# Decode tokens that follow the prompt through out-projection and MLP of a hybrid decoder step

## The chip, the cores and the metric

The kernel runs on one core of one Trainium2 chip. The metric is the device time of one execution in microseconds (us), the median of several runs. It is an inference step of a two-layer decoder for a prompt of 512 tokens and 8 decode tokens at once, with the same weights.

## The reference, cut to what matters

Both groups of tokens pass the same layers. The change lies in layer 0: the mixers' output is multiplied by `w_out`, added to the residual behind a norm, and followed by an MLP with a squared ReLU.

```python
def even_mixer(h, w_in, ..., w_out, lam_init, gla_s0, attend):
    ...
    a_out = rmsnorm(attend(da_q, da_k, da_v), g_da) * (1.0 - lam_init)
    ...
    o = rmsnorm(o.astype(h.dtype), g_gla) * jax.nn.silu(g_og).reshape(B, T, GLA_HEADS, GLA_DV)
    mix = jnp.concatenate([a_out.reshape(B, T, DA_V), o.reshape(B, T, GLA_V)], axis=-1)
    return (mix @ w_out).astype(h.dtype), da_k, da_v, s_new.astype(h.dtype)
...
def sq_relu_mlp(h, w_up, w_down):
    return jnp.square(jax.nn.relu(h @ w_up)) @ w_down
...
        yp = yp + rmsnorm(mp, g[1])
        ys = ys + rmsnorm(ms, g[1])
        yp = yp + rmsnorm(sq_relu_mlp(rmsnorm(yp, g[2]), w_up[layer], w_down[layer]), g[3])
        ys = ys + rmsnorm(sq_relu_mlp(rmsnorm(ys, g[2]), w_up[layer], w_down[layer]), g[3])
```

`attend` of a decode token reads a paged cache of 4096 past keys and values (`diff_attn_sample`), 128 MB over the 8 tokens: 64 chunks of 1 MB of keys and 64 of values. D_MODEL is 1024, the MLP's inner width 4096, all of it fp32.

## The kernel before, in words

Activations lie with the features on the 128 partitions (8 tiles of features, `KT`) and the tokens in columns: T = 520, the prompt's 512 and behind them the 8 decode tokens. A large product runs in chunks of weights of 1 MB (1024 x 256), each with two tiles of 128 output features. A weight is split in two parts that the fast fp32r matmul takes, `W_hi` (ACT, `split_hi`, L810) and `W_lo` (DVE, `split_lo`, L1285), the activations likewise into `H_hi` and `H_lo` (in the MLP's second product `U_hi` and `U_lo`), and a tile adds W_hi·hi, W_hi·lo and W_lo·hi for 8 k tiles. As a PSUM bank holds 512 columns, each of these is two matmuls of 260 columns in two banks: 48 matmuls in a tile (`step`, L1876 to 1883):

```python
for n, (w, x) in enumerate(((W_hi, hi), (W_hi, lo), (W_lo, hi))):
    for j, half in enumerate(halves):
        t = MM_(PS[:, 2 * bank + j, 0:HALF], w[:, ch.slot, k, cols], x[:, k, half],
                start=k == 0 and n == 0, stop=k == KT - 1 and n == 2)
```

The chunks follow each other: 13 of the input projection, C_OUT0 with 4 of the out-projection (8 tiles), C_MLP0 with 32 of the first MLP (64 tiles, in four groups of four up and four down chunks), C_IN1 with 8, C_OUT1 with 4 and C_MLP1 with 32 of layer 1. They come by SP's queue (`RAW`). In front of the MLP stands an opening, in which tiles already run in quarters while the norm of the residual is made.

The program is written engine by engine, with semaphores between them, and each engine's order is the order of the code. Work is laid in between by numbered slots (`slot`): the prompt's attention is 16 units, GLA 8 units, and the page cache is worked on in between. `load_order` makes one list of 128 loads of it, k chunks and v chunks: `UNIT_STEPS` says how many k chunks an attention unit takes (with two v chunks), `GLA_STEPS` the same for a GLA unit (three v chunks each). POOL issues these loads as indirect DMAs (L747) into a ring of six 1 MB buffers `KV` once the chunk that lay there is used. A k chunk costs DVE three passes (a product, L1364, and two sums, L1352 and L1366) and POOL a product (L680); a v chunk is four fp32 matmuls of 32 x 512 on four column groups of PE (`v_chunks`, L2074), with weights `PM` that POOL copies (L693) from the softmax scores; its use increments `v_used`. POOL further makes the powers of the norms (`power`, L704 and L708) and zeroes `ACC`. SP brings back the residual X (2 MB, put aside while two of the six buffers lie in its place) once `v_used` is at 62, ahead of a load of the out-projection's weights.

After the GLA units the tail follows: the last v chunks, the decode tokens' softmax sums (`smz_done`), Exp on ACT, the past output (`past_output`), squares, their sum (`new_sq`), the root (`new_root`) and the split of the decode tokens' columns into H_hi and H_lo. PE waits for it (`new_ready`) in front of the out-projection.

## Time and profile before

| | us |
|---|---|
| median of 3 runs | 1544.59 |
| lowest and highest run | 1537.25, 1545.81 |
| profiled execution, span from first to last instruction | 1541.8 |
| PE busy (matmuls) in it | 1406.3 |
| DVE, ACT, POOL busy | 882.3, 516.7, 328.7 |

No separate time is given for the profiled execution: its span stands for it, and lies 2.8 us under the median. A busy PE is an engine that has a matmul in it, not one at its peak. The two stretches of the change are the units of attention and GLA (190 to 515 us), and out-projection with MLP (540 to 971 us).

### The profile page before, as it was taken

To read this page: it belongs to the slowest core of one execution; us is meant where nothing else is said; L and a number is where in the kernel's file an instruction comes from. 1 tells how busy PE (TensorE), PEld (TensorE's weight loads), DVE (VectorE), ACT (ScalarE), POOL (GpSimd) and SP (SyncE) were. 2 spreads that over 40 slices of the span, in tenths; PEclk is the share of its full clock that TensorE was granted. 3 is DMA by queue.
4 is the path that set the end of the run, shared out by engine and by line. 5 is a ranking of instruction groups with operands and counts; after the bars stand their busy time and mean duration, and the time that the engine had idled before them with its cause. 6 is when DMAs were issued, how large, how long until landed. Compare 5 with 4: busy or idle time off the path is not lost.

```text
span 1541.8 us, 26106 instructions
## 1 busy us (share of the span) xinstructions
PE 1406.3 (91%) x11324; PEld 1266.3 (82%) x11324; DVE 882.3 (57%) x1156; ACT 516.7 (34%) x839; POOL 328.7 (21%) x264
## 2 busy tenths in 40 slices
PE   4999957788778698999999999899989999999997
PEld 3999933345334398999999999899989999999997
DVE  3398978766988526624435343689556344353443
ACT  3323254433423424312212122469443122131233
POOL 1085768865777100000000000000000000000000
PEclk8999979877676799999999999999999999999999
DMA  9477699988989831232322322222212323223211
GB/s 320 137 264 232 236 327 382 369 324 326 346 322 346 300 109 55 86 106 83 97 97 82 99 94 83 83 83 83 85 55 88 105 83 101 92 83 103 90 55 56
DMA packets 126856, 249.32 MB, mean 162 GB/s; under 512 B 5251, under 2 KB 107415, under 8 KB 110096
## 3 DMA queue, kind: packets, MB, share of 16 engines
q0 software_dynamic: 18432, 134.23, 22.9%
q1 hardware_dynamic: 103616, 107.13, 21.5%
q10 hardware_dynamic: 4696, 6.32, 1.3%
q8 instruction: 89, 1.46, 0.4%
q14 instruction: 23, 0.19, 0.0%
HBM read 239.99 MB, written 7.73 MB: 161 GB/s over the span
## 4 chain that ended last, share of the span: by engine, by line
PE 58%; issue 25%; DVE 7%; POOL 4%; DMA 3%; ACT 3%; ACTq 0%; POOLq 0%; DVEq 0%
PE PS L1881 46%; PE PS L2074 2%; POOL PROD L680 2%; DMA KV<-in_cache_v,CIDX 2%; DVE SC L1352 1%; PE PS L2216 1%; POOL KV L747 1%; DVE ST L1584 1%; PE PS L2061 1%; PE PS L2158 1%; DMA XSIN<-in_x_sample 1%; PE PS L1865 1%; PE PS L2179 1%; PE PS L2116 1%; PE PS L1975 1%
## 5 line engine op out<-in xcount | busy, mean ns | idle before, releaser
L1881 PE MATMUL PS<-H_hi,W_hi 128*128 128x260 f32 x1936 | 397.7, 287 | 16.7 <-DVE H_lo L1327 9.7
L1881 PE MATMUL PS<-H_hi,W_lo 128*128 128x260 f32 x1936 | 393.4, 285 | 0.0
L1881 PE MATMUL PS<-H_lo,W_hi 128*128 128x260 f32 x1936 | 393.0, 285 | 0.0
L1881 PEld LDWEIGHTS PS<-H_hi,W_hi 128*128 128x128 f32 x1936 | 303.2, 191 | 22.3 <-issue 17.7
L1881 PEld LDWEIGHTS PS<-H_hi,W_lo 128*128 128x128 f32 x1936 | 301.9, 191 | 0.0
L1881 PEld LDWEIGHTS PS<-H_lo,W_hi 128*128 128x128 f32 x1936 | 301.7, 191 | 0.0
L1285 DVE TENSOR_TENSOR W_lo<-RAW,W_hi 128x2048 fp32r<-128x2048 f32 x90 | 208.2, 2313 | 125.9 <-ACT W_hi L810 125.8
L810 ACT ACTIVATE W_hi<-RAW 128x2048 fp32r<-128x2048 f32 x90 | 171.8, 1909 | 266.1 <-PE PS L1881 265.5
L1881 PE MATMUL PS<-U_hi,W_lo 128*128 128x260 f32 x1024 | 206.4, 283 | 0.0
L1881 PE MATMUL PS<-U_lo,W_hi 128*128 128x260 f32 x1024 | 206.0, 283 | 0.0
L1881 PE MATMUL PS<-U_hi,W_hi 128*128 128x260 f32 x1024 | 206.0, 282 | 0.0
L680 POOL TENSOR_TENSOR PROD<-KV,QB 128x1024 f32<-128x1024 f32 x64 | 152.0, 2375 | 120.4 <-DVE SC L1352 91.5
L1717 DVE TENSOR_TENSOR ACC<-ACC,PS 128x520 f32<-128x520 f32 x64 | 44.6, 697 | 201.4 <-PE PS L1881 201.4
L1881 PEld LDWEIGHTS PS<-U_hi,W_hi 128*128 128x128 f32 x1024 | 157.9, 189 | 0.0
L1881 PEld LDWEIGHTS PS<-U_hi,W_lo 128*128 128x128 f32 x1024 | 157.9, 188 | 0.0
L1881 PEld LDWEIGHTS PS<-U_lo,W_hi 128*128 128x128 f32 x1024 | 157.4, 188 | 0.0
L753 POOL MEMSET ACC<- 128x4160 f32 x2 | 7.1, 3572 | 637.3 <-DVE TMP L1310 637.3
L1124 ACT ACTIVATE UF<-SQ 128x520 f32<-128x520 f32 x64 | 40.8, 639 | 253.2 <-DVE SQ L1683 253.2
L2074 PE MATMUL PS<-KV,PM 128*32 128x512 f32 x512 | 88.2, 777 | 23.4 <-DMA KV<-in_cache_v,CIDX 13.6
L1683 DVE SCALAR_TENSOR_TENSOR SQ<-PS,RS 128x520 f32<-128x520 f32 x64 | 44.6, 700 | 109.2 <-PE PS L1881 109.2
L1364 DVE TENSOR_TENSOR PROD<-KV,PS 128x1024 f32<-128x1024 f32 x64 | 77.5, 1210 | 9.0 <-ACT QB L866 8.9
L747 POOL DMA_INDIRECT KV<-in_cache_k,CIDX x64 | 70.4, 1100 | 53.8 <-DVE TMP L1310 23.1
(304 smaller groups left out, 1433.8 us busy)
## 6 DMA issues: line engine op xcount, KB each, us to landing
RAW<-in_w_up SPq DMA_DIRECT2D x32, 1024.0 KB
RAW<-in_w_down SPq DMA_DIRECT2D x32, 1024.0 KB
...
```

Of the source, the lines that this page charges most:

```text
L680: nc.gpsimd.tensor_tensor(PROD[:, 1], KV[i % RING][:, 2:4, :], QB[:, None, b % 2, :].to_broadcast([P, 2, 512]), ALU.mult).then_inc(prod1_r ...
L747: po.indirect_dma_start(KV[i % RING].rearrange("p n f -> p (n f)"), None, cache[kind], bass.IndirectOffsetOnAxis(ap=CIDX[:, n:n + 1], axis ...
L810: A(W_hi[:, ch.slot], RAW[:, ch.slot], ACT.Copy).then_inc(w_hi_ready, 1)
L1124: A(UF[:, i], RL[:, i], ACT.Square).then_inc(uf_ready, 1)
L1285: V.tensor_tensor(W_lo[:, ch.slot], RAW[:, ch.slot], W_hi[:, ch.slot].bitcast(F32), ALU.subtract).then_inc(w_lo_ready, 1)
L1352: V.tensor_reduce(k_scores(n, 1), PROD[:, 1].rearrange("p n (j d) -> p n j d", d=DH), AX.X, ALU.add).then_inc(prod1_used, 1)
L1364: V.tensor_tensor(PROD[:, 0], KV[i % RING][:, 0:2, :], PS[:, None, 6 + b % 2, :].to_broadcast([P, 2, 512]), ALU.mult).then_inc(k_used, 1)
L1584: V.scalar_tensor_tensor(ST[:, hp, state(tb, n + 1)], ST[:, hp, state(tb, n)], DECC[:, hp, 8 * tb + n:8 * tb + n + 1], update(n, slice(0, ...
L1683: V.scalar_tensor_tensor(pair(RL[:, i]), tile_banks(ch, i), 0.0, pair(RS[:, 1]), ALU.max, ALU.mult).then_inc(banks_free[ch.par[i]], 1)
L1717: V.tensor_tensor(pair(ACC[:, m]), pair(ACC[:, m]), banks(ch.par[i]), ALU.add).then_inc(banks_free[ch.par[i]], 1)
L1881: t = MM_(PS[:, 2 * bank + j, 0:HALF], w[:, ch.slot, k, cols], x[:, k, half], start=k == 0 and n == 0, stop=k == KT - 1 and n == 2)
L2074: t = MM_(PS[32 * pos:32 * pos + 32, 4, :], PM[:, part % 2, at:at + 32], KV[i % RING][:, pos, :], start=n % 32 == 0, stop=n % 32 == 31)
```

## The change

The prompt passes the out-projection and the first MLP alone. A tile of the chunks from C_OUT0 up to C_IN1 (`prompt_only`, 72 tiles) has 24 matmuls of 512 columns into one bank; splits and evictions of these chunks leave the decode tokens' columns out. The decode tokens follow behind the tiles of the MLP (`sample(t)`, with t the tile, on PE, ACT and DVE): t=4 softmax sums and past output, 5 attention, 7 and 8 norm, 10 and 11 four chunks of `w_out`, 13 fold, 15 to 19 norms, and from t=21, with a period of 8, per group four up chunks (behind two tiles), a fold, and four down chunks, at the end a fold and the residual (behind tiles 53 to 56). A chunk is 8 fp32 matmuls with the tokens' values as weights of 32 columns (8 tokens, four times) and 256 columns of the model's weights (`sample_products`, L2169), on four column groups of PE; `folds` adds up the four and turns them back to features on partitions (8 matmuls of 128 x 128 by 8 columns). POOL loads these weights again, 36 chunks of 1 MB in rows of 1 KB by `dma_start` (L814), into a ring of three buffers; a load waits until the chunk before in its buffer is used (`w_used`). SP restores X once the last cache chunks that lie in its place (v 48 and 49) are used.

The cache's chunks are spread anew: in the attention units by turns 1 and 2 k chunks (8 more), in the GLA units by turns 2 and 1 (12 in place of 20) with two v chunks each (16 in place of 24), then v chunks 48 to 51, and 52 to 63 in pairs behind the first six tiles of the out-projection (`values_behind`). The weights `PM` have a second buffer. POOL zeroes ACC ahead of the fourth weight load.

PE's order in front of the out-projection. Before: the last two v chunks, the past output's sums (L2082), the norm's sum (L2197) and the first tile, which waits for `new_ready`.

```order
L2074 MATMUL PS<-KV_69,PM 32x512 [waits pm_ready,kv_loaded0]
L2074 MATMUL PS<-KV_69,PM 32x512 x3
L2074 MATMUL PS<-KV_69,PM 32x512 [waits pm_ready,kv_loaded1]
L2074 MATMUL PS<-KV_69,PM 32x512 x3
L2082 MATMUL PS<-CONST,OG_111 128x32 [waits og_copied]
L2082 MATMUL PS<-CONST,OG_111 128x32 x3
L2197 MATMUL PS<-MM,ONES 128x64 [waits new_sq,hf_ready,gs_v_used]
L1881 MATMUL PS<-H_hi,W_hi 128x260 [waits banks_free1,h_ready,w_lo_ready,new_ready]
L1881 MATMUL PS<-H_hi,W_hi 128x260
L1881 MATMUL PS<-H_lo,W_hi 128x260 x2
L1881 MATMUL PS<-H_hi,W_lo 128x260 x2
```
In the change PE has v chunks 50 and 51 there, the last norm of GLA (L2359), and then the tile, without that wait and 512 columns wide.

```order
L2344 MATMUL PS<-KV_69,PM_99 32x512 [waits pm_ready,kv_loaded0]
L2344 MATMUL PS<-KV_69,PM_99 32x512 x3
L2344 MATMUL PS<-KV_69,PM_99 32x512 [waits pm_ready,kv_loaded1]
L2344 MATMUL PS<-KV_69,PM_99 32x512 x3
L2359 MATMUL PS<-NDG,OT 128x128 [waits nd_ready,gs_v_used,st_ready]
L2359 MATMUL PS<-NDG,OT 128x128 [waits nd_ready]
L2086 MATMUL PS<-H_hi,W_hi 128x512 [waits h_ready,banks_free1,w_lo_ready]
L2086 MATMUL PS<-H_lo,W_hi 128x512
L2086 MATMUL PS<-H_hi,W_lo 128x512
```
The past output and the norm's sum stand behind tiles of the MLP now. In the out-projection two v chunks lie between two tiles:

```order
L2086 MATMUL PS<-H_hi,W_hi 128x512 [waits h_ready]
L2086 MATMUL PS<-H_lo,W_hi 128x512
L2086 MATMUL PS<-H_hi,W_lo 128x512
L2344 MATMUL PS<-KV_69,PM_99 32x512 [waits pm_ready,kv_loaded2]
L2344 MATMUL PS<-KV_69,PM_99 32x512 x3
L2344 MATMUL PS<-KV_69,PM_99 32x512 [waits pm_ready,kv_loaded3]
L2344 MATMUL PS<-KV_69,PM_99 32x512 x3
L2086 MATMUL PS<-H_hi,W_hi 128x512 [waits banks_free0]
L2086 MATMUL PS<-H_lo,W_hi 128x512
```
And in the MLP two chunks of `w_up` between two tiles, L2169, with XH as the tokens' values:

```order
L2086 MATMUL PS<-H_hi,W_lo 128x512
L2086 MATMUL PS<-H_hi,W_hi 128x512
L2086 MATMUL PS<-H_lo,W_hi 128x512
L2086 MATMUL PS<-H_hi,W_lo 128x512
L2169 MATMUL PS<-KV_69,XH 32x256 [waits kv_loaded0,operand_ready]
L2169 MATMUL PS<-KV_69,XH 32x256 x7
L2169 MATMUL PS<-KV_69,XH 32x256 [waits kv_loaded1]
L2169 MATMUL PS<-KV_69,XH 32x256 x7
L2086 MATMUL PS<-H_hi,W_hi 128x512 [waits banks_free0]
L2086 MATMUL PS<-H_lo,W_hi 128x512
```
These are each behind a wait on the load, and the first also on the tokens' values (`operand_ready`).

DVE's order in the attention units, before (a k chunk is L1352, L1364, L1366):

```order
L1546 RECIPROCAL RR<-SM 128x2 [waits ex_done]
L1520 TENSOR_TENSOR PR<-PS,BIAS 128x1024 [waits at_done,sc_done]
L1523 TENSOR_REDUCE MX<-PR 128x2 [waits sc_used]
L1529 TENSOR_SCALAR OTC<-PS 128x128 [waits o_copied]
L1538 SCALAR_TENSOR_TENSOR NRS<-NSQ,NRS 128x1 [waits root_done]
L1352 TENSOR_REDUCE SC_78<-PROD 128x2x8 [waits prod1_ready]
L1364 TENSOR_TENSOR PROD<-KV_70,PS 128x1024 [waits kv_loaded5]
L1366 TENSOR_REDUCE SC_78<-PROD 128x2x8 [waits k_used]
L1404 TENSOR_REDUCE ROWSUM<-SC_77 128x8 [waits soft_done,dve_step]
L1546 RECIPROCAL RR<-SM 128x2 [waits ex_done]
```
and in the change, in a unit that takes two (the lines are L1472, L1484 and L1486):

```order
L1666 RECIPROCAL RR<-SM 128x2 [waits ex_done,dve_step]
L1640 TENSOR_TENSOR PR<-PS,BIAS 128x2x128 [waits at_done,sc_done]
L1643 TENSOR_REDUCE MX<-PR 128x2 [waits sc_used]
L1649 TENSOR_SCALAR OTC<-PS 128x128 [waits o_copied]
L1658 SCALAR_TENSOR_TENSOR NRS<-NSQ,NRS 128x1 [waits root_done]
L1472 TENSOR_REDUCE SC_78<-PROD 128x2x8 [waits prod1_ready]
L1484 TENSOR_TENSOR PROD<-KV_70,PS 128x1024 [waits kv_loaded5]
L1486 TENSOR_REDUCE SC_78<-PROD 128x2x8 [waits k_used]
L1472 TENSOR_REDUCE SC_78<-PROD 128x2x8 [waits prod1_ready,dve_step]
L1484 TENSOR_TENSOR PROD<-KV_69,PS 128x1024 [waits kv_loaded0]
L1486 TENSOR_REDUCE SC_78<-PROD 128x2x8 [waits k_used]
L1472 TENSOR_REDUCE SC_78<-PROD 128x2x8 [waits prod1_ready,dve_step]
```
DVE's third pass of one k chunk is followed by the three of the next, ahead of the unit's next step.

The diff, cut:

```diff
     IN_STEPS, PRE_STEPS = 2, (3, 3)
-    UNIT_STEPS = [1] * 16
-    GLA_STEPS = [3, 3, 3, 3, 3, 3, 2, 0]
+    UNIT_STEPS = [1, 2] * 8
+    GLA_STEPS = [2, 1] * 4
     GLA_SLOT = len(UNIT_STEPS) + 13
+    OUT_SLOT = GLA_SLOT + 17
...
-            take("kvkvkv" if n == 3 else "kvkvv" if n == 2 else "vvv")
+            take("kvkv" if n == 2 else "kvv")
...
-        return order
+        return order + [("w", n) for n in range(36)]
...
+    ALL_SIX, SAMPLE_RING = 114, 3
+
+    def buffer(i):
+
+        return i % RING if i < ALL_SIX else (i - ALL_SIX) % 4 if i < LOADS else (i - LOADS) % SAMPLE_RING
...
+    def prompt_only(ch):
+
+        return C_OUT0 <= ch.static < C_IN1
...
-                sp.wait_ge(v_used, 62)
+                for i in range(ALL_SIX - RING, ALL_SIX):
+                    if BUFFER[i] >= 4:
+                        freed(sp, i)
                 sp.dma_start(X[:].rearrange("p k t -> p (k t)"), xsave).then_inc(x_saved, 16)
...
+        def sample_weights(n):
+
+            if n < 4:
+                return stage_dram(a["w_out_even"][0], 0, slice(256 * n, 256 * n + 256))
+            c, j = SAMPLE_CHUNKS[n - 4]
+            if c[0] == "up":
+                return stage_dram(a["w_up"][0], 0, slice(1024 * c[1] + 256 * j, 1024 * c[1] + 256 * j + 256))
+            return a["w_down"][0].rearrange("(q r p) n -> p q r n", p=P, r=KT)[:, c[1], :, 256 * j:256 * j + 256]
+
+        used = 0
+        for i, (kind, n) in enumerate(ORDER):
+            if (kind, n) == ("w", SAMPLE_RING):
+                zero_acc(0)
+            if BEFORE[i] is not None:
+                while used <= BEFORE[i]:
+                    use(used)
+                    used += 1
...
+            if kind == "w":
+                po.dma_start(weights_of(n), sample_weights(n)).then_inc(kv_loaded[BUFFER[i]], 16)
+            else:
+                po.indirect_dma_start(KV[BUFFER[i]].rearrange("p n f -> p (n f)"), None, cache[kind],
+                                      bass.IndirectOffsetOnAxis(ap=CIDX[:, n:n + 1], axis=0)).then_inc(kv_loaded[BUFFER[i]], 16)
...
             for n, (w, x) in enumerate(((W_hi, hi), (W_hi, lo), (W_lo, hi))):
+                if prompt_only(ch):
+                    t = MM_(PS[:, bank, :], w[:, ch.slot, k, cols], x[:, k, 0:SEQ], start=k == 0 and n == 0, stop=k == KT - 1 and n == 2)
+                    continue
                 for j, half in enumerate(halves):
...
+        def sample_products(n, op, bank, fresh):
+
+            i = place("w", n)
+            pe.wait_ge(kv_loaded[BUFFER[i]], LANDED[i])
+            for r in range(2):
+                for c in range(4):
+                    k = 4 * r + c
+                    t = MM_(PS[32 * c:32 * c + 32, bank, 256 * (n % 2):256 * (n % 2) + 256], op[:, k], weights_of(n)[:, k],
+                            start=fresh and r == 0, stop=r == 1, skip_group_check=True)
+            t.then_inc(w_used, 1)
+
+        def folds(n):
+
+            pe.wait_ge(part_copied, min(2 * n + 1, 10))
+            for k in range(KT):
+                t = MM_(PS[:, 6, 64 + 8 * k:72 + 8 * k], SE[:, P * k:P * k + P], FOLD[:, 0:8], start=True, stop=True)
+            t.then_inc(fold_done, 1)
...
+            if t in (10, 11):
+                pe.wait_ge(operand_ready, 1)
+                for n in range(2):
+                    sample_products(2 * (t - 10) + n, XM, 3 if t == 10 else 5, True)
...
+            g, at = group_step(t)
+            if at in (0, 1):
+                pe.wait_ge(operand_ready, 2)
+                for n in range(2):
+                    sample_products(4 + 8 * g + 2 * at + n, XH, 2 + 2 * at, True)
+            if at == 3:
+                folds(g + 1)
+            if at in (5, 6):
+                pe.wait_ge(operand_ready, g + 3)
+                for n in range(2):
+                    sample_products(4 + 8 * g + 4 + 2 * (at - 5) + n, XU[:, g % 2], 3 if at == 5 else 5, g == 0 and n == 0)
...
+        v_chunks(48, 4)
         pe.wait_ge(st_ready, 64)
-        pe.wait_ge(k_used, 64)
-        v_chunks(56, 2)
-        normalise(23)
-        pe.wait_ge(ssum_ready, 8)
...
-        v_chunks(58, 6)
-        past_output(1)
-
-        pe.wait_ge(gs_v_used, N_SAMPLE)
...
-        pe.wait_ge(new_ready, 1)
-        stage(C_OUT0, 4, 1)
+        pe.wait_ge(gs_v_used, N_SAMPLE)
+        normalise(23)
+
+        def values_behind(t):
+
+            slot(OUT_SLOT + t)
+            if t < 6:
+                v_chunks(52 + 2 * t, 2)
+
+        stage(C_OUT0, 4, 1, values_behind)
```

## Rows read from the trace of the kernel before

**Rows 1.** Busy time by stretch (us, x instructions), PE clock, DMA share, GB/s.
```profile
core 0: us, PE busy (x) PEld busy (x) DVE busy (x) ACT busy (x) POOL busy (x), PEclk, DMA share, GB/s
190.00:366.00 176.00, 133.16 (x754) 72.14 (x754) 130.72 (x188) 76.86 (x223) 127.68 (x114) 0.81 0.91 347
366.00:515.00 149.00, 114.93 (x851) 60.08 (x854) 120.09 (x216) 51.26 (x174) 102.06 (x91) 0.69 0.91 342
515.00:540.20 25.20, 13.73 (x82) 5.53 (x74) 16.11 (x44) 11.47 (x25) 3.89 (x6) 0.72 0.71 247
540.20:618.90 78.70, 73.68 (x672) 72.57 (x673) 33.99 (x39) 27.69 (x40) 3.57 (x1) 0.94 0.25 78
618.90:970.90 352.00, 351.99 (x2932) 351.86 (x2936) 151.12 (x160) 86.69 (x77) 0.00 (x0) 1.00 0.28 91
```

**Rows 2.** The chain of waits from the out-projection on: start us, us, what.
```profile
540.22 47.72 PE PS L1881 x384
...
618.91 351.99 PE PS L1881 x2928
```

**Rows 3.** Costliest groups of DVE, 190 to 366 us, shapes apart.
```profile
L1366 DVE TENSOR_REDUCE SC<-PROD 128x16 f32<-128x1024 f32 x23 | 28.1, 1221 | 0.8
L1364 DVE TENSOR_TENSOR PROD<-KV,PS 128x1024 f32<-128x1024 f32 x23 | 27.8, 1210 | 0.0
L1352 DVE TENSOR_REDUCE SC<-PROD 128x16 f32<-128x1024 f32 x22 | 26.7, 1214 | 1.4 <-POOL PROD L680 1.4
```

**Rows 4.** Waits of DVE, 190 to 366 us: total us, times, longest.
```profile
DVE PR L1520 <- PE PS L2061: 23.8, 10, 5.1
```

**Rows 5.** Busy time by stretch, the stretch in which the DMA is fullest.
```profile
224.00:296.00 72.00, 53.56 (x325) 25.44 (x323) 58.36 (x85) 34.47 (x115) 56.84 (x55) 0.89 0.97 378
```

**Rows 6.** The chain of waits, GLA units: start us, us, what.
```profile
374.35 3.71 PE PS L2158 x32
...
393.46 7.75 DMA KV<-in_cache_v,CIDX
...
468.47 1.93 PE PS L2158 x16
...
483.14 8.06 DMA KV<-in_cache_v,CIDX
...
503.67 1.93 PE PS L2158 x16
```

**Rows 7.** Timeline of the tail, 528 to 540.5 us: start us, us, engine, line.
```profile
528.03 0.69 DVE L1609 TENSOR_TENSOR H_lo<-HTMP,H_hi 128x512 fp32r<-128x512 f32 x1
...
529.99 1.89 ACT L810 ACTIVATE W_hi<-RAW 128x2048 fp32r<-128x2048 f32 x1
...
535.68 2.28 DVE L1285 TENSOR_TENSOR W_lo<-RAW,W_hi 128x2048 fp32r<-128x2048 f32 x1
```

**Rows 8.** The chain of waits, a gate product of layer 1.
```profile
1007.54 1.75 PE PS L2216 x8
```

**Rows 9.** The chain of waits, a v chunk and a small product.
```profile
342.08 0.99 PE PS L2074 x8
343.08 1.87 PE PS L2044 x16
```

**Rows 10.** The view of DMA issues: median us from issue to landing.
```profile
KV<-in_cache_v,CIDX POOLq DMA_INDIRECT x64, 8.0
```

**Rows 11.** Groups from 366 to 515 us: POOL's issue of a cache load.
```profile
L747 POOL DMA_INDIRECT KV<-in_cache_v,CIDX x28 | 27.8, 994 | 8.0 <-POOL PROD L680 3.5 <-PE PS L2074 2.1 <-issue 1.7
```

**Rows 12.** DMA queues of the page: packets, MB, share of 16 engines.
```profile
q0 software_dynamic: 18432, 134.23, 22.9%
q1 hardware_dynamic: 103616, 107.13, 21.5%
```

**Rows 13.** Groups of DVE from 618.9 to 970.9 us.
```profile
L1688 DVE CAST U_hi<-UF 128x520 fp32r<-128x520 f32 x32 | 13.8, 431 | 20.5 <-ACT UF L1124 20.4
```

More of the change, by code:

```diff
@@ L523, in trunk, with weights_of, group_step @@
     LOADS = 128
+    ALL_SIX, SAMPLE_RING = 114, 3
+    def buffer(i):
+        return i % RING if i < ALL_SIX else (i - ALL_SIX) % 4 if i < LOADS else (i - LOADS) % SAMPLE_RING
+    BUFFER = [buffer(i) for i in range(len(ORDER))]
+    BEFORE = [max([j for j in range(i) if BUFFER[j] == BUFFER[i]], default=None) for i in range(len(ORDER))]
+    LANDED = [16 * BUFFER[:i + 1].count(BUFFER[i]) for i in range(len(ORDER))]
+    def weights_of(n):
+        return KV[BUFFER[place("w", n)]].rearrange("p n f -> p (n f)").rearrange("p (k n) -> p k n", k=KT)
+    SAMPLE_CHUNKS = [((what, g), j) for g in range(4) for what in ("up", "down") for j in range(4)]
+    SAMPLE_MLP, SAMPLE_PERIOD = 21, 8
+    SAMPLE_END = SAMPLE_MLP + 3 * SAMPLE_PERIOD + 6
+    def group_step(t):
+        g, at = divmod(t - SAMPLE_MLP, SAMPLE_PERIOD)
+        return (g, at) if 0 <= g < 4 and t >= SAMPLE_MLP else (None, None)
     UNITS = [(h, qb) for h in range(HEADS) for qb in range(4)]
@@ L685, in weights @@
             b, half = divmod(part, 2)
+            PM = PM_AT[part // 8]
             if part == 0:
@@ new lines, in part, with fold_square @@
+        def part(n, banks_):
+            act.wait_ge(w_used, 4 if n == 0 else 36 if n == 9 else 8 * ((n - 1) // 2) + 6 + 2 * ((n - 1) % 2))
+            if n >= 1:
+                act.wait_ge(fold_done, (n + 1) // 2)
+            for i, bank in banks_:
+                t = A(SE[:, 512 * i:512 * i + 512], PS[:, bank, :], ACT.Copy)
+            t.then_inc(part_copied, 1)
+        def fold_square(n, src):
+            if n >= 1:
+                act.wait_ge(new_summed, n + 1)
+            A(by_tile(E1), src, ACT.Square).then_inc(new_sq, 1)
@@ L2202, in _ @@
         mlp(0, C_MLP0, 2)
+        pe.wait_ge(sample_moved, 4)
         sum_squares(3)
```

416 lines of the change are left out of this document (271 added, 145 removed).

## The prediction

> **What bounds the kernel now.** I read the busy time by stretch first, then the chain of waits, then the groups. Over the two stretches in which the change makes PE's tiles narrower PE never rests: 73.7 of 78.7 us and 351.99 of 352.0 us, with DVE at 151 of 352 and DMA at 0.28 [rows 1]. The chain says the same: 47.72 us for the 384 matmuls of the out-projection's 8 tiles, then 351.99 us in one piece for 2928 matmuls, 61 tiles [rows 2]. So a microsecond of PE work added or removed there is a microsecond of the kernel, and all other engines have room. From 190 to 515 us it is otherwise: PE is busy 133 of 176 and 115 of 149 us, DVE 131 and 120, POOL 128 and 102, DMA 0.91 of its time, in both [rows 1]. No engine is full; the units of attention and GLA are chains through PE, ACT and DVE, and the page cache's chunks (one k chunk costs three DVE passes and one POOL product) are laid in between. From 515 to 540.2 us there is the tail, where PE waits for the decode tokens' softmax, norm and split.
>
> **The change, part by part.**
>
> *Attention units, +16.* Eight units take one k chunk more. A chunk costs DVE 1.22 + 1.21 + 1.21 = 3.64 us [rows 3], eight of them 29. DVE waits there 23.8 us in 10 waits for scores of PE [rows 4], half of which or a little more the new work can fill: +14 by DVE, +29 if nothing is absorbed. By DMA: 8.4 MB more, at the 378 GB/s of the fullest stretch [rows 5] 22 us, less what the share still leaves (0.91 against 0.97 of 176 us, 11 us): +11. With some friction between the two I take **+16**, bounds +11 and +29.
>
> *GLA units, −31.* The first stretch of state products starts at 374.35, that of the sixth unit at 468.47, that of the eighth at 503.67 [rows 6]: 18.8 us for a unit with 3 k and 3 v chunks, and 35.2 for one such and the one with 2 and 2 (16.4 for the latter; by one chunk's DVE time less, 18.8 − 3.64, it would be 15.2, and I take 15). The last, with none, needs 515 − 503.67 = 11.3. A unit with one k chunk is put at 12.5, between 11.3 and 15. Before: 515 − 366 = 149, of which 8.4 lie ahead of 374.35. Now 8.4 + 4 × 15 + 4 × 12.5 = 118: **−31**. The chain has waits on a v chunk's DMA of 7.75 and 8.06 us there [rows 6], which fall due to fewer chunks in the queue; that speaks for more (−38), a unit that can't get under 14 for less (−20).
>
> *Tail, −8.* PE started the out-projection at 540.22 [rows 2]. The prompt's last H_lo is done at 528.72; then ACT began W_hi late (529.99 for 1.89) and DVE W_lo at 535.68 for 2.28, behind the decode tokens' chain [rows 7]. Now the wait on that chain is gone from PE's first row of the out-projection. 528.7 − 0.7 (ACT is free when DVE does the last H_lo) + 1.9 + 2.3 = 532.2: **−8**, bounds −6 and −11 (the last norm's square roots come earlier on ACT, but four v chunks stand on PE before them).
>
> *Tiles 24 × 512, −41.* A matmul of 260 columns takes 351.99/2928 = 0.1202 us, so a pair 0.2404. What does one of 512 columns take? The nearest row is the fp32 gate product of layer 1: 8 records in 1.75 us, 0.219 each [rows 8], and such a record streams its 260 columns twice, 520. Per column that is 0.421 ns, so 512 take 0.2155. The other bound is that the 260s pay per column (0.1202/260 × 512 = 0.2367). I take 0.2155, since the row with as many columns gives it. 72 tiles × 24 × (0.2404 − 0.2155) = 43; two of the three opening tiles wait anyway, **−41**. Bounds −6 and −43. The Trainium skill, "TensorE: Matmul & The Clock Gate", section "Wait — 56ns, not 53.3ns?", says a matmul costs N/2.4 GHz and some 2.5 ns more. The row of the 260s disagrees, 120.2 against 110.8 ns. By the rule a tile would now take 24 × 215.8 = 5.18 us, as I have it, but before 48 × 110.8 = 5.32, and the saving would be 10 us, not 41.
>
> *48 chunks between tiles, +48.* Twelve v chunks move from ahead of the out-projection to behind its tiles, and 36 chunks of re-read weights (4 out-projection, 16 up, 16 down) are new, each with 8 fp32 matmuls of 32 × 256 on four column groups at once. PE's order shows both kinds between tiles, each behind a wait on its load. A v chunk standing alone takes 0.99 us at full clock [rows 9]; a weight chunk has 16 records, four side by side, so four rounds of 512 streamed columns at 0.2155: 0.86, and its end drains like the other's. 48 × 0.99 = **+48**; 48 × 0.86 = 41 is the lower bound.
>
> *Folds and small sums, +14.* A fold is 8 fp32 matmuls, 16 records, with a full weight load and 8 columns. 16 records of that sort (64 × 128 weights, one column) took 1.87 us [rows 9]; six folds +11, and the softmax sums, the past output's sums and the four norm sums **+3**.
>
> *Loads of the re-read weights, +3.* The ring has three buffers, a four of chunks is used by two tiles in a row. The fourth chunk takes the buffer of the first, which comes free behind tile t and is wanted behind tile t+1 and the third chunk: 1.0 + 5.2 + 1.0 = 7.2 us later. A v chunk lands 8.0 us after its issue (median) [rows 10], POOL's issue costs 1.0 [rows 11]; by that each of nine fours would be 1.8 us late, +16. But those loads shared the DMA at 0.91, while here it stands at 0.28; alone, the weight queue needs 21.5% × 1541.8/107.13 = 3.1 us of all engines for one MB [rows 12], which leaves 4 us for issue and what lies around the transfer; so I take most of them in time: **+3**, bounds 0 and +16. POOL has nothing else to do there; the zeroing of ACC is put ahead of the fourth load, long before its use. SP's restore of X waited for v chunk 62 and now for v 48 and 49; it stands ahead of w_out loads in SP's queue and comes earlier. Edits at nothing: DVE's and ACT's decode work between tiles (small operations, 64 columns wide), under PE with DVE idle 200 of 352 us; if a tile's eviction came behind such a step by more than a tile's time (5.2 us) it would cost. The Trainium skill, "SBUF — State Buffer", section "SBUF: two separate sides", warns that a load issued from GpSimd stands still while DVE runs an fp32 SBUF-to-SBUF copy. Such copies run in the MLP, 32 of U_hi at 0.43 us [rows 13]; no row shows whether they hold a load up. By the page each four could be late by one of them, 9 × 0.43 = 4 us more than my sum, and it adds to B's chance.
>
> **Sum.** Front +16 − 31 − 8 = −23. PE stretch −41 + 48 + 14 + 3 = +24. Together +1; against the traced execution 1541.8 + 1 = 1543. That span lies 2.8 under the median of the runs, 1544.59; I forecast **1544**, for the median.
>
> **Rivals.**
> *A, the front gives more* (1529). The attention units take their chunks for +11, GLA falls by 38, the tail by 11: −38, with +24 behind it −14. For it: two DMA waits of 8 us each in the GLA chain, with fewer chunks to fetch. Against: of DVE's 120 us of work in GLA 20 × 3.64 = 73 are chunks, and not all of that is on the chain.
> *B, loads late* (slower, 1557 to 1596). POOL's issue costs 1.0 us for a cache chunk whose packets are 134.23 MB/18432 = 7.3 KB; the weight queue's are 107.13 MB/103616 = 1.0 KB [rows 12], so a chunk of weights has seven to eight times as many. If POOL pays by the piece, 7.8 us an issue, a group's eight chunks need 63 us of POOL, while its 8 tiles and 8 chunks take PE 50: +13 for each of four groups, +52 (1596). If only landing is as the cache's, +16, so +13 against my sum (1557). It decides from issue and landing over 7.2 us. For it: nothing in the trace has POOL issuing small rows. Against: slack elsewhere in the ring.
> *C, attention pays in full* (1557): DVE's 29 us land in the chain since the waits it could fill are at the wrong units: +13.
> *D, columns alone set PE's price* (1579): a tile saves 0.09 us, not 0.58.
> *E, nothing of it bites* (1544): gains and costs go unseen, the opening of the MLP or another wait swallowing both.
>
> **How the numbers follow.** Half a per cent, 7.7 us, is about what a measurement tells from no change. The forecast's case has 0.42: its terms wander by some 9 us around +0, so 0.15 faster, 0.22 same, 0.05 slower. A 0.24, all faster. B 0.14 and D 0.05, slower. C 0.09, of which 0.03 same. E 0.06, same. Faster 0.39, same 0.31, slower 0.30. The rule on the clock's page, by which the tiles save 10 and not 41, would give 1575; I give it 0.01 of D's 0.05, since the row of the 260s says otherwise. The range holds the forecast's own (1530 to 1557), A's with its bounds and B's and C's lower parts: 1521 to 1568.
>
> **What would show it.** Tiles of 24 matmuls at 5.17 us, 0.2155 a piece, under MLP 0; at 0.2367 a piece D is right. PE between two tiles at 0.9 to 1.0 us per chunk, with no wait on KV of the weights; B would show as waits of PE on the DMA of w_up or w_down, or as POOL busy for microseconds at each issue. The stretch of attention units 158 us long with DVE at nine tenths; GLA's starts of state products 15 and 12.5 us apart in turn; the out-projection starting near 517. The forecast is wrong if MLP 0 with the out-projection is not some 24 us longer, or the front not some 23 us shorter.

## The result and the profile after

The changed kernel takes 1589.49 us (median of 4 runs, 1586.40 to 1592.71) against 1542.71 us for the kernel before: the ratio is 1.0305, 95% interval 1.0279 to 1.0331. It is 47 us slower than before and 45 us over the forecast of 1544, whose range went up to 1568. The profiled execution has a span of 1586.1 us, so 44.3 us more than that of before.

The chain of waits of the changed kernel shows where PE's time goes now (start us, us, what; L2086 is the tile's matmuls, L2169 a chunk of re-read weights, L2177 a fold):

```profile
531.51 8.52 PE PS L2086 x24
634.25 16.83 PE PS L2086 x72
668.06 1.86 PE PS L2169 x32
669.93 5.79 PE PS L2086 x24
688.95 1.68 PE PS L2177 x16
771.02 7.37 DMA KV<-in_w_down
826.05 8.21 DMA KV<-in_w_down
936.63 8.03 DMA KV<-in_w_down
970.25 44.71 PE PS L2086 x192
1014.96 1.95 PE PS L2070 x64
```

The out-projection starts at 531.51, not at 540.22, and the MLP's end (the norm's first sum, L2070) comes at 1014.96, not 970.90 [rows 2]. So in these two profiles the front (all that stands ahead of the out-projection) gave 8.7 us, and out-projection and MLP took 483.5 us in place of 430.7, 52.8 more, where 24 were forecast; the rest of the program is as long as it was (571.1 and 570.9 us). Three tiles in a row take 16.83 us, eight take 44.71: 5.6 us each, 0.233 us a matmul of 512 columns. That is the row to keep in mind: the sum had 0.2155.

Busy time by stretch, with the columns of [rows 1]:

```profile
190.00:366.00 176.00, 124.49 (x639) 65.04 (x637) 143.29 (x194) 71.73 (x204) 133.88 (x116) 0.76 0.93 348
531.50:1015.00 483.50, 476.34 (x2664) 362.69 (x2668) 195.05 (x253) 126.02 (x141) 48.55 (x47) 0.99 0.53 174
```

PE is busy 476 of 483.5 us: still the bound, as before. DVE from 190 to 366 us rose from 131 to 143 of 176 us, and its waits for scores stayed (from 190 to 390 us, as the attention units end 28 us later):

```profile
DVE PR L1640 <- PE PS L2331: 21.6, 10, 5.4
```

23.8 us before [rows 4], 21.6 now in the longer stretch, 10 waits in both: the added k chunks did not fill them. The loads of the re-read weights, by the page's view of DMA issues (KB each, median us to landing) and POOL's timeline (start us, us):

```profile
KV<-in_w_up POOLq DMA_DIRECT2D x16, 1024.0 KB, 7.7
KV<-in_w_down POOLq DMA_DIRECT2D x16, 1024.0 KB, 8.3
```

```profile
771.02 0.88 POOL L814 DMA_DIRECT2D KV<-in_w_down  x1 [24.31 <-PE PS L2169]
```

POOL's issue of a load in rows of 1 KB costs 0.88 us here and at most 1.00 in any of the 36, no more than one of the cache's [rows 11]. Landing takes 7.7 to 8.3 us (medians of `w_up` and `w_down`) against the 7.2 that the ring leaves, and PE waits for it in three places.

### The profile page after: what moved, and what is told of

Its sections match the earlier page's. It is cut to its first block, busy times and chain, and to the rows that moved or that the text cites. A ratio compares the mean times of both kernels' runs of the same rounds, so it can differ in the third digit from the quotient of the medians.

```text
span 1586.1 us, 24121 instructions
## 1 busy us (share of the span) xinstructions
PE 1446.0 (91%) x10274; PEld 1201.7 (76%) x10274; DVE 886.8 (56%) x1184; ACT 527.3 (33%) x858; POOL 363.1 (23%) x301
## 4 chain that ended last, share of the span: by engine, by line
PE 56%; issue 25%; DVE 9%; POOL 4%; ACT 3%; DMA 3%; POOLq 0%; ACTq 0%; DVEq 0%
PE PS L2086 24%; PE PS L2089 18%; PE PS L2344 3%; POOL PROD L724 3%; PE PS L2169 2%; DVE SC L1472 2%; DMA KV<-in_w_down 1%; DVE ST L1704 1%; PE PS L2428 1%; PE PS L2483 1%; PE PS L2177 1%; PE PS L2245 1%; POOL KV L816 1%; DVE SC L1486 1%; PE PS L2070 1%
## 5 line engine op out<-in xcount | busy, mean ns | idle before, releaser
L2089 PE MATMUL PS<-H_hi,W_hi 128*128 128x260 f32 x1296 | 267.0, 288 | 10.0 <-DVE H_lo L1447 6.5
L2089 PE MATMUL PS<-H_hi,W_lo 128*128 128x260 f32 x1296 | 263.4, 285 | 0.0
L2089 PE MATMUL PS<-H_lo,W_hi 128*128 128x260 f32 x1296 | 263.3, 285 | 0.0
L1919 DVE TENSOR_TENSOR ACC<-ACC,PS 128x512 f32<-128x512 f32 (+1 forms) x64 | 44.3, 692 | 202.5 <-PE PS L2089 103.3
L2086 PE MATMUL PS<-H_hi,W_hi 128*128 128x512 f32 x320 | 130.6, 408 | 15.5 <-DVE W_lo L1405 12.1
L2086 PE MATMUL PS<-H_hi,W_lo 128*128 128x512 f32 x320 | 128.0, 400 | 0.0
L2086 PE MATMUL PS<-H_lo,W_hi 128*128 128x512 f32 x320 | 127.5, 398 | 0.0
L1884 DVE SCALAR_TENSOR_TENSOR SQ<-PS,RS 128x512 f32<-128x512 f32 (+1 forms) x64 | 44.3, 695 | 116.1 <-PE PS L2086 61.3
L2089 PE MATMUL PS<-U_hi,W_lo 128*128 128x260 f32 x512 | 103.2, 283 | 0.0
L2089 PE MATMUL PS<-U_lo,W_hi 128*128 128x260 f32 x512 | 103.0, 283 | 0.0
L2089 PE MATMUL PS<-U_hi,W_hi 128*128 128x260 f32 x512 | 103.0, 282 | 0.0
L2086 PE MATMUL PS<-U_hi,W_hi 128*128 128x512 f32 x256 | 102.6, 401 | 0.0
L2086 PE MATMUL PS<-U_hi,W_lo 128*128 128x512 f32 x256 | 101.3, 396 | 0.0
L2086 PE MATMUL PS<-U_lo,W_hi 128*128 128x512 f32 x256 | 100.8, 394 | 0.0
```

What stands on the lines that cost most here:

```text
L1884: V.scalar_tensor_tensor(tile_cols(ch, RL[:, i]), tile_banks(ch, i), 0.0, tile_cols(ch, RS[:, 1]), ALU.max, ALU.mult).then_inc(banks_free[ ...
L1919: V.tensor_tensor(tile_cols(ch, ACC[:, m]), tile_cols(ch, ACC[:, m]), tile_banks(ch, i), ALU.add).then_inc(banks_free[ch.par[i]], 1)
L2086: t = MM_(PS[:, bank, :], w[:, ch.slot, k, cols], x[:, k, 0:SEQ], start=k == 0 and n == 0, stop=k == KT - 1 and n == 2)
```

## The experiments

Twelve kernels ran. The theory after the result (P): an fp32r matmul of 512 columns costs 233 ns, not 215.5, and this alone is 72 x 24 x 17.5 ns = 30 us, about all of what the stretch took beyond its forecast (52.8 against 24). The rivals: late loads (B, as in the prediction), and the added traffic slowing PE's matmuls (called C in this section; it is not the prediction's C, attention in full).

**What a matmul costs, alone.** `e1_widths_alone` puts sections of 96 matmuls behind PE's last work in the kernel before:

```diff
+        def w_of(i):
+            return WT[:, P * (i % 16):P * (i % 16) + P]
+
+        def x_of(i, n):
+            return XT[:, 512 * (i % 7):512 * (i % 7) + n]
...
+        for i in range(96):
+            MM_(PS[:, bank(i), :], w_of(i), x_of(i, 512), start=first(i), stop=last(i))
...
```

`WT` and `XT` are `W_hi` and `W_lo` flattened; `bank(i)` changes every 24 matmuls.

> The kernel before, with eleven sections of 96 matmuls each behind PE's last work, all other engines idle. A new 128x128 weight load stands before each. Theory P (an fp32r matmul pays 0.449 ns a column and 3.4 ns more, from 120.0 ns at 260 and 233 ns at 512 in the traces): 512 columns 233 ns in all fp32r sections of that width, whichever bank they write, 384 columns 176, 260 columns 120, 256 columns 118, 128 columns 61. Rival Q (the 512s are slow since one bank takes matmul upon matmul): 233 with one bank for 24 in a row, 216 with banks by turns. Rival C (the other engines or the DMA slow PE's reads or writes): 216 in all sections of 512 here, since all else is idle. The fp32 section (256 columns, two passes) at 108 a record and the bf16 section at 216 would say that it is the fp32r form that costs, 233 in bf16 that it is the width. The time of the whole is before's plus some 200 us and says nothing.

The timeline of PE (start us, us from the first start to the last end, form, count); a section's starts lie 96 apart from the next one's:

```profile
1571.05 21.92 PE L2280 MATMUL PS<-W_lo,W_hi 128*128 128x512 f32 x96
1592.81 21.92 PE L2282 MATMUL PS<-W_lo,W_hi 128*128 128x512 f32 x96
1614.57 16.83 PE L2284 MATMUL PS<-W_lo,W_hi 128*128 128x384 f32 x96
1631.24 11.67 PE L2286 MATMUL PS<-W_lo,W_hi 128*128 128x256 f32 x96
1642.74 11.56 PE L2288 MATMUL PS<-W_lo,W_hi 128*128 128x260 f32 x96
1654.14 10.83 PE L2290 MATMUL PS<-W_lo,W_hi 128*128 128x128 f32 x96
...
1686.67 41.60 PE L2294 MATMUL PS<-W_lo,W_hi 128*128 128x256 f32 x192
1728.33 20.67 PE L2296 MATMUL PS<-XBF,WBF 128*128 128x512 bf16 x94
1748.64 22.12 PE L2298 MATMUL PS<-W_lo,W_hi 128*128 128x512 f32 x96
```

(1592.81 − 1571.05)/96 = 0.2267 us at 512 columns, in one bank as with banks by turns (L2282): rival Q falls. 384 columns cost (1631.24 − 1614.57)/96 = 0.1736, 256 cost 0.1199, 260 cost 0.1187, 128 cost 0.111, where theory P had 0.061 for the last. From 256 to 512 that is 0.417 ns a column, full speed, and 13.4 ns on top of N/2.4: on these rows theory P's form (nearly all by the column) falls. But 13.4 ns isn't a constant of every width: at 260 columns only 10.4 ns lie on top, at 128 it is 58. Nor is it there at the lower clock: the starts of the first section (L2278) lie 427 ns apart while its granted clock is 0.50 (1.2 GHz), which is 512/1.2.

The fp32 product has two records a matmul, 192 in all, and they start 0.216 us apart (median), twice the 108 that I expected; 256 columns in a record of fp32 so take the time of 512 in a bf16 matmul, also 0.216. So at 512 streamed columns it is the fp32r form that pays; my row for the price, an fp32 product [rows 8], was of a kind that doesn't. 0.2267 is still not 0.233: 6 ns were open.

**The rest of it: where the moving rows start.** `e8_operands_alone` takes the tile's operands apart:

```diff
+            MM_(PS[:, bank(i), :], w_of(i), XT[:, 520 * (i % 6):520 * (i % 6) + 512], start=first(i), stop=last(i))
...
+            MM_(PS[:, bank(i), :], (W_hi, W_hi, W_lo)[i % 3][:, 1, (i // 3) % KT, P:2 * P], (U_hi, U_lo, U_hi)[i % 3][:, (i // 3) % KT, 0:512], start=first(i), stop=last(i))
```

> The kernel before with seven sections of 96 fp32r matmuls of 512 columns behind PE's last work, all else idle: which part of the operands takes them from 226.7 ns (first run) to the 233 of the tiles. In order: as in the first run (226.7); the moving rows 2080 bytes apart, not 2048; weights taken in rows of 1024 bytes out of W_hi; the tile's own order of weights (W_hi twice, then W_lo) with moving rows from W_hi; that order with the tile's own moving tiles (U_hi, U_lo, U_hi); plain weights with U_hi's rows; the same tile in rows 2048 bytes apart. Theory A (addresses of the moving rows): 233 in the second, fifth and sixth, 227 in the last. Theory W (the weights' order or layout): 233 in the third, fourth and fifth. Theory N (what else runs on the chip): 227 everywhere.

```profile
1550.74 24.55 PE L2280 MATMUL PS<-W_lo,W_hi 128*128 128x512 f32 x96 [13.56 <-ACT WBF L1250]
1575.12 22.46 PE L2282 MATMUL PS<-W_lo,W_hi 128*128 128x512 f32 x96
1597.42 21.94 PE L2284 MATMUL PS<-W_lo,W_hi 128*128 128x512 f32 x96
```

Rows 2080 bytes apart: (1597.42 − 1575.12)/96 = 0.2323. The mean spacing of the seven sections, from the trace: 227 (the median; this section begins at the lower clock), 232.2, 226.9, 232.2, 232.5, 234.1, 226.9 ns. Theory A holds: the second, the fifth and the sixth are slow, the last (the same U_hi, rows of 2048 bytes) is not. The fourth is slow too, but its moving rows also lay 2080 bytes apart, so it says of the weights' order only that it adds nothing to the second. Weights' layout and order do nothing that shows, and all this with everything else idle, so nothing is left for other engines.

`e9_addresses_alone` moves the start of rows 2048 bytes apart, by s = 4, 8, 16, 32, 64, 128 and 256 columns of 4 bytes:

```diff
+            MM_(PS[:, bank(i), :], w_of(i), XT[:, 512 * (i % 6) + 4:512 * (i % 6) + 516], start=first(i), stop=last(i))
...
```

> The kernel before with fourteen sections of 96 fp32r matmuls behind PE's last work, all else idle. First as in the first run (512 columns, moving rows 2048 bytes apart: 226.7 ns). Then the same rows moved by 16, 32, 64, 128, 256, 512 and 1024 bytes. If the price hangs on the start's alignment, the sections up to some power of two stand at 229 to 237 and the rest at 227: at 64 bytes and more if rows of 64 bytes matter, only at 1024 if it is larger blocks. If instead all stand at 227, it is not the start but that starts differ from one matmul to the next (rows 2080 bytes apart) that costs. Then six sections of pairs with the same weights, in two banks: 260 + 260 in rows of 2080 bytes as the kernel before has them (120 expected each, as there), 256 + 256 aligned (119.9 if the fixed part holds), 260 twice from the same aligned start (118.7 as in the first run), 260s at rows of 2112 and starts of 1056 bytes, 260s at rows of 2176 and starts of 1024 bytes, and 264s at 1024 in rows of 2080. Differences over 1 ns in the 260s would be worth 90 x 2 x 48 x 1 ns = 8 us to the kernel before.

```profile
1572.03 22.40 PE L2282 MATMUL PS<-W_lo,W_hi 128*128 128x512 f32 x96
1594.27 22.57 PE L2284 MATMUL PS<-W_lo,W_hi 128*128 128x512 f32 x96
1616.67 22.14 PE L2286 MATMUL PS<-W_lo,W_hi 128*128 128x512 f32 x96
1638.65 22.46 PE L2288 MATMUL PS<-W_lo,W_hi 128*128 128x512 f32 x96
1660.95 21.93 PE L2290 MATMUL PS<-W_lo,W_hi 128*128 128x512 f32 x96
1682.71 21.92 PE L2292 MATMUL PS<-W_lo,W_hi 128*128 128x512 f32 x96
...
1726.23 11.68 PE L2296 MATMUL PS<-W_lo,W_hi 128*128 128x260 f32 x96
1737.75 11.68 PE L2298 MATMUL PS<-W_lo,W_hi 128*128 128x256 f32 x96
1749.27 11.55 PE L2300 MATMUL PS<-W_lo,W_hi 128*128 128x260 f32 x96
1760.66 11.70 PE L2302 MATMUL PS<-W_lo,W_hi 128*128 128x260 f32 x96
1772.20 11.79 PE L2304 MATMUL PS<-W_lo,W_hi 128*128 128x260 f32 x96
1783.83 12.00 PE L2306 MATMUL PS<-W_lo,W_hi 128*128 128x264 f32 x96
```

Shifted by 16, 32, 64 and 128 bytes: 231.6, 233.4, 228.9, 232.3 ns; by 256, 512 and 1024: 226.7. So a start at a multiple of 256 bytes, counted from the beginning of `W_lo`, is free, and each other one that was tried costs 2 to 7 ns. For the 260s of the kernel before it is another story: in rows of 2080 bytes 120.0 ns, both halves from the same aligned start 118.7, and the two layouts meant to be better 120.2 and 121.1. The aligned 256s take 120.0, more than the aligned 260s; why is open. A 260 + 260 in 2080 is within 1.3 ns of the best that was tried.

`e11_before_aligned` asked this of the whole kernel before:

```diff
-                    t = MM_(PS[:, 2 * bank + j, 0:HALF], w[:, ch.slot, k, cols], x[:, k, half],
+                    t = MM_(PS[:, 2 * bank + j, 0:HALF], w[:, ch.slot, k, cols], x[:].rearrange("p k t -> p (k t)")[:, 512 * k + 256 * j:512 * k + 256 * j + HALF],
```

> The kernel before with the moving operand of every tile's matmuls taken from windows of 260 columns that begin 1024 bytes apart (512k and 512k + 256 of the flattened tile, so partly other tokens' and features' numbers), in all chunks. If the 260s pay for their starts as the 512s do (227 against 233), up to 1.3 ns a matmul (118.7 idle and aligned against 120.0 in the tiles): 8640 x 1.3 = 11 us less than before, 1531. If a 260's 120 ns has nothing to do with addresses: no change, 1542.

1558.85 us, ratio 1.0117 (1.0089 to 1.0145): 16 to 18 us slower, a miss of both theories. The chain has the MLP's piece at

```profile
619.50 357.69 PE PS L1881 x2928
```

0.1222 a matmul against 0.1202. What in these windows costs it (they overlap, and each starts 1024 bytes after the last) is open. It does say that where the moving windows lie can cost this kernel 1%.

`e10_rows_2048` lays out the moving tiles of the prompt-only products in rows of 2048 bytes:

```diff
+    HP_hi, HP_lo = (sb(n, [P, KT, SEQ], F32R, at) for n, at in (("HP_hi", r_h), ("HP_lo", r_h + KT * TB)))
+    UP_hi, UP_lo = (sb(n, [P, KT, SEQ], F32R, at) for n, at in (("UP_hi", r_1), ("UP_lo", r_1 + KT * TB)))
```

> The changed kernel with the moving tiles of the prompt-only products (both halves of H and U) laid out in rows of 512 columns, 2048 bytes apart and starting on 256 bytes, not in rows of 520; nothing else differs. If the start addresses cost what the idle sections show (233 against 226.7 ns at 512 columns), a tile falls from 5.60 to 5.44 us and the whole by 72 x 24 x 6.3 ns = 11 us from the changed kernel's 1589.5, to 1579. If what else runs on the chip makes the 6 ns, tiles stay at 5.60 and the time at 1589.

1584.78 us (ratio to before 1.0273, 1.0221 to 1.0326). The chain:

```profile
641.48 16.45 PE PS L2091 x72
...
971.44 43.62 PE PS L2091 x192
```

A tile takes 5.45 to 5.48 us where it took 5.6; the median spacing of its matmuls under MLP 0 is 227 ns, where it was 232. From the out-projection's start to the MLP's end it is 475.4 us against 483.5, 8 us less. The tiles show the effect of the rows; the whole shows 5 of the expected 11, and the rest is within what the front (below) wanders.

**The width alone.** `e2_before_wide` is the kernel before with the wide tiles (and one matmul more in the opening's third tile, for the bank that it would leave empty):

```diff
+                if C_OUT0 <= ch.static < C_IN1:
+                    t = MM_(PS[:, 2 * bank, :], w[:, ch.slot, k, cols], x[:, k, 0:SEQ], start=k == 0 and n == 0, stop=k == KT - 1 and n == 2)
+                    if bank == THIRD and k == 0 and n == 0:
+                        MM_(PS[:, 2 * bank + 1, 0:HALF], w[:, ch.slot, k, cols], x[:, k, 0:HALF], start=True, stop=True)
+                    continue
```

> The kernel before with the change's wide tiles alone: 24 matmuls of 512 columns in the 72 tiles of out-projection and MLP 0. The decode tokens' columns of these tiles are left out, and nothing is put in their place. Theory P: a tile falls from 5.77 to 5.60 us, 72 x 0.17 = 12 us less than before, about 1530. The prediction's price (0.2155 us a matmul): 5.17 a tile, 41 us less, about 1501.

```profile
543.87 46.66 PE PS L1881 x192
...
620.54 340.64 PE PS L1881 x1464
```

1532.27 us, 0.993 of before (0.990 to 0.996), 10 us less; the MLP's piece fell from 351.99 to 340.64 [rows 2], and from the out-projection's start to the MLP's end it is 417.3 us in place of 430.7. So the price of 0.233 is right for the tile without the change's other parts (340.64/1464), and on rows of 2080 bytes the width gives 10 to 13 us, not 41. Some 6 of them (72 x 24 x 8/2.4 ns, an estimate from full speed by the column) are the eight columns that a pair no longer has. `e7_halves_one_bank` cuts the matmuls in two in the changed kernel:

```diff
+                    for j in range(2):
+                        t = MM_(PS[:, bank, 256 * j:256 * j + 256], w[:, ch.slot, k, cols], x[:, k, 256 * j:256 * j + 256], start=k == 0 and n == 0 and j == 0, stop=k == KT - 1 and n == 2 and j == 1)
```

> The changed kernel with each matmul of 512 columns cut into two of 256, in the same bank. If each fp32r matmul pays a fixed 13.4 ns beside N/2.4 (first run: 226.7 ns at 512, 173.6 at 384, 119.9 at 256, all idle), a tile takes 48 x 0.1199 = 5.76 us or a little more, against 5.60: 72 x 0.16 = 12 us more than the changed kernel, 1601. If the cost goes by the column (theory P of the first run), 48 x 0.1184 = 5.68, 6 us more, 1595. If the 6 ns that the tiles' 512s take beyond the idle 226.7 come from the length of a single matmul, the halves stand at 0.1165 and nothing is lost: 1589.

```profile
639.61 17.05 PE PS L2087 x144
```

1598.48 us, 9 us over the changed kernel; three tiles in 17.05, 5.68 each, 0.1184 a half. That is the tile of the second case, cost by the column, to the last digit, and not the 5.76 of a fixed 13.4 ns. So the numbers of the idle sections on aligned rows don't carry over to these tiles: on rows of 2080 bytes a pair of 256s (236.8) costs only 3.4 ns more than one 512 (233.4), on aligned rows 13 ns more (2 x 119.9 against 226.7). The time, 9 us more, lies between the two cases. Why a 256 isn't slowed by the starts that slow a 512 is open.

**The decode tokens' products and their loads.** `e3_no_weight_loads` and `e4_half_products`:

```diff
-                po.dma_start(weights_of(n), sample_weights(n)).then_inc(kv_loaded[BUFFER[i]], 16)
...
-            pe.wait_ge(kv_loaded[BUFFER[i]], LANDED[i])
```

> The changed kernel without the 36 loads of re-read weights and PE's waits on them; the decode tokens' products run on what lies in the buffers (so their out-projection and MLP of layer 0 are computed from other data). Theory P: tiles stay at 5.60 us, only PE's waits on late loads go, 3 to 4 us: 1586. Rival B (late loads hold the kernel up): 10 us or more less, under 1580. Rival C (the added DMA traffic slows PE's matmuls): tiles near 5.2 us, 30 us less, 1560.

1589.67 us: no gain. From the out-projection's start to the MLP's end it is 480.2 us against 483.5. Of these 3.3 us, 1.4 are the first tile (7.16 against 8.52; its matmuls start 427 ns apart while the granted clock is 0.50, 12 of them in the changed kernel and 5 here, and near 232 ns after). From the MLP's fourth tile on it is 391.3 us against 393.7, so the waits on late loads were worth 2.4 us, near the sum's +3; whatever DVE's copies of U_hi did to these loads is in that. The tiles stayed at 5.6 us with the DMA at 0.30 of its time in place of 0.53:

```profile
540.49 7.16 PE PS L2084 x24
...
540.50:1020.70 480.20, 475.16 (x2664) 362.62 (x2668) 195.00 (x253) 126.03 (x141) 15.93 (x11) 0.99 0.30 97
```

B and C both fall. A gain of 2 us can't be told from nothing in the time: the four runs lie between 1586 and 1594, and in the profiles the front ended at 540.5 here and at 531.5 in the changed kernel.

```diff
-            for r in range(2):
+            for r in range(1, 2):
                 for c in range(4):
...
-                            start=fresh and r == 0, stop=r == 1, skip_group_check=True)
+                            start=fresh, stop=True, skip_group_check=True)
```

> The changed kernel with 4 of the 8 matmuls of each re-read chunk (the other half of the inner dimension is left out of the decode tokens' products). If a chunk costs what its matmuls stream (two rounds of four records at 0.215 us gone of four), 36 x 0.43 = 15.5 us less than the changed kernel, 1574. If a chunk's price is mostly that PE's run of tiles is broken, under 8 us less, over 1581.

```profile
679.16 7.70 DMA KV<-in_w_out_even
...
745.81 1.00 PE PS L2169 x16
746.81 5.79 PE PS L2086 x24
```

1579.41 us, 10 us less, between the two cases. From the out-projection's start to the MLP's end it is 473.1 us, 10.4 less. A pair of chunks fell from 1.86 to 1.00, as priced (18 pairs, 15.5 us), but a third of that came back: PE now waits longer for loads (5.0 us in PE's own waits, against 1.7). With shorter products the ring's buffers are wanted sooner, which would explain it; no run tests that. The 5.79 behind a pair, against 5.6 in a row, is the break: 0.19 us a time.

**The front.** `e5_tables_back` puts eight k chunks back from the attention into the GLA units:

```diff
-    UNIT_STEPS = [1, 2] * 8
-    GLA_STEPS = [2, 1] * 4
+    UNIT_STEPS = [1] * 16
+    GLA_STEPS = [3, 3, 3, 3, 3, 2, 2, 1]
```

> The changed kernel with the k chunks where they were: one in every attention unit, and 3, 3, 3, 3, 3, 2, 2, 1 in the GLA units (20), the v chunks as in the change. If a k chunk costs DVE's 3.64 us on the chain wherever it lies (rival C of the prediction, for both stretches), attention falls by 28 us and GLA rises by 28 to 29: the changed kernel's time within 3 us, 1589. If GLA has more room than attention, its eight chunks cost 15 to 20 us there, and the whole falls to 1577 to 1582. If DVE's waits fill with the chunks in attention only, it rises to 1595 or more.

1581.45 us, 8 us less (ratio to before 1.0261, 1.0222 to 1.0299), as in the second case. In its profile the first mask of GLA is written at 366.9 in place of 401.4 (373.5 in before), and from there to the last unit's it takes 121.9 us in place of 101.8. One profile of each isn't enough here, since the front wanders; more are at hand, as other runs have the same front. Means, in us from the profiles:

| front | profiles | first mask of GLA | from it to the last unit's | from there to the out-projection | out-projection's start |
|---|---|---|---|---|---|
| of before | before, e1, e2, e8, e9 | 372.1 (369.6 to 374.4) | 129.6 (127.5 to 131.6) | 39.1 | 540.8 (537.9 to 543.9) |
| of the change | changed kernel, e3, e4, e7, e10 | 402.3 (401.3 to 403.2) | 105.9 (101.8 to 108.8) | 29.5 | 537.7 (531.5 to 541.7) |
| of e5 | e5, e12 | 370.4 (366.9, 374.0) | 122.0 (121.9, 122.0) | 30.9 | 523.3 (519.7, 526.8) |

So a k chunk cost (402.3 − 370.4)/8 = 4.0 us in attention, all of DVE's 3.64 and more, and (122.0 − 105.9)/8 = 2.0 in GLA. The stretches, the changed kernel's first, then e5's:

```profile
222.00:366.00 144.00, 106.42 (x548) 52.46 (x548) 118.28 (x165) 53.80 (x178) 111.96 (x103) 0.76 0.95 356
401.50:503.00 101.50, 80.50 (x680) 44.88 (x676) 78.64 (x152) 41.84 (x146) 58.24 (x52) 0.75 0.73 272
```

```profile
222.00:366.00 144.00, 115.62 (x688) 60.33 (x688) 110.25 (x172) 64.10 (x214) 110.54 (x109) 0.86 0.96 367
366.90:488.80 121.90, 85.90 (x685) 48.25 (x685) 108.51 (x182) 45.02 (x150) 84.78 (x69) 0.68 0.81 299
```

DVE is busy for 0.77 of the thinned GLA and 0.89 with the chunks back, and for 0.82 of attention with the added chunks and 0.77 without. These shares alone don't tell which stretch has room: 0.77 in both, and a chunk costs twice as much in attention. My reading is that DVE, ACT and PE wait for each other in each attention unit, so that what is laid between delays all of it; no run tests that reading by itself.

`e6_w_hi_early` moves ACT's split in the tail of the kernel before:

```diff
         squares_of(23)
+        split_hi(Chunk(C_OUT0))
         normalise(23)
...
         A(E2[:], E2[:], ACT.Exp).then_inc(mm_exp, 1)
-        split_hi(Chunk(C_OUT0))
```

> The kernel before with one thing moved in its tail: ACT makes W_hi of the out-projection's first chunk behind the squares of the last GLA unit, not between the decode tokens' Exp and the past output's copy. In the chain of before it holds 1.8 us there. Expected 1.8 us less than before, 1540 to 1541, which three rounds will hardly tell from nothing; the trace must show the past output's copy right behind Exp and the out-projection's start 1.8 us sooner after the clamp.

```profile
517.52 1.89 ACT L810 ACTIVATE W_hi<-RAW 128x2048 fp32r<-128x2048 f32 x1
...
531.41 0.24 ACT L1060 ACTIVATE E<-E 128x64 f32<-128x64 f32 x1
...
532.05 0.60 ACT L997 ACTIVATE OG<-PS 128x512 f32<-128x512 f32 x1 [0.40 <-PE PS L2074]
```

1539.34 us, 0.998 of before (0.9958 to 1.0002): the split has left the chain, and from the last GLA unit's mask to the out-projection it is 36.8 us in place of 38.6, the 1.8 expected (38.4 to 40.0 in four more profiles with the front of before). In the time it can't be told from nothing. Of the versions that leave nothing out it is the only one that isn't slower than before; no run found one that is clearly faster.

`e12_rows_and_tables` joins e10 and e5:

```diff
+    HP_hi, HP_lo = ...
-    UNIT_STEPS = [1, 2] * 8
+    UNIT_STEPS = [1] * 16
```

> The two mended together: rows 2048 bytes apart, and the k chunks back in the GLA units as in e5. The savings lie in different stretches and should add: 11 for the rows and 8 for the tables, 1589.5 - 19 = 1570. If the front's saving was chance (e5's front in its profile was 12 us shorter, its median 8), only the rows' part remains, 1579. Both stand clear above the 1542 of the kernel before, because the 36 re-read chunks, the folds and the twelve v chunks stay on PE.

```profile
628.57 16.45 PE PS L2091 x72
```

1575.91 us (1.021 of before, 1.0154 to 1.0266), 13.6 us under the changed kernel: the two add up, 5 and 8 as each alone gave, and so stay 6 short of the 1570 expected, all of it on the side of the rows. It stays 33 us over before.

## Why the prediction was wrong

*Tiles, −41: the step that failed.* The direction was right (one matmul in place of two costs less), the size was off by three to four times. The row that I took by its columns, the gate product, was fp32, and the tiles are fp32r: 512 columns cost 226.7 ns on aligned rows, 233 on rows of 2080 bytes, not 215.5. Measured worth of the width: 10 us in the time of e2, 13 in its stretch. These 29 or so are the larger part of the 45 us by which the time missed. The other bound, 236.7 ns, from the 260s' price by the column, was 3 ns off, and rival D, with 0.05, came closest to what happened. Its price by the column is nearly right for these tiles, as e7 shows, and not in general: on aligned rows a wide matmul saves 13 ns against two of 256, and the addresses of the rows take back half of that. The rule of the Trainium skill, "TensorE: Matmul & The Clock Gate", section "Wait — 56ns, not 53.3ns?", of N/2.4 GHz and 2.5 ns more, agrees with bf16 here (216 ns against 215.8) and with the fp32 records, not with fp32r. By that rule the saving would be 10 us, which hit the measured one, but by luck in part: both of its prices are too low, by 9 ns at 260 columns and 17 at 512. I had weighed the 260s' row against the rule and not asked whether the other row was of the same type.

*48 chunks, +48.* Right: a pair 1.86 and 0.19 for the break, 24 times 2.05 is 49. *Folds and sums, +14*: six folds of 1.68 and some 2 us, about 12. *Loads, +3*: right, 2.4 by e3; POOL's issue (B's 7.8 us) is 0.88.

*Attention, +16: the second step that failed.* It took 28.0 in the profile and 30 on the mean of five, the upper bound: rival C, for which I had 0.09. The chain's rows of waits on scores looked like room and weren't: they stayed at 21.6 us with eight chunks more. Why they stay is argued above, not shown. *GLA, −31, and tail, −8*: −26.4 and −10.2 in the profile, which together is near the −39 of the sum, but by luck, as it was the fastest GLA of the five. On the mean they gave −24 and −10 (between the masks of first and last unit, and from there to the out-projection). A unit takes 15.1 us on the mean (105.9/7), where I had 15 and 12.5 by turns, 13.75. No start of a unit lies less than 12.6 us behind the one before, and on the mean of five the gaps are 13.4 to 17.2, not in step with the chunks; what else fills them is open.

The front's end isn't a fixed number: with the same program it lies between 531.5 and 541.7. The table shows where it wanders: attention ends within 2 us in all five, GLA takes 101.8 to 108.8. What makes GLA wander is open; between the changed kernel's and e4's the granted clock of PE there differs a little (0.75 and 0.73, same stretch), and no run tells it apart. On the mean the change's front gives 3 us, with some 2 of doubt by the spread, not the forecast's 23 (or rival A's 38) and not the 8.7 of its own profile.

So: front −3, tiles −12 (with the out-projection's), chunks +49, folds and sums +12, late loads +2, together +48, against 46.8 measured and +1 forecast. Two terms carry the miss: the tiles by 29 us and the front by 20. The forecast went wrong on its least certain term: a gain of 41 us that rested on one row of another data type, against costs of 65 us that were sure.
